# Sample attention of a decoder step: which load is asked for first, products side by side in the array, and the LayerNorm's columns

## What is computed

```python
q, k, v = project(x, w_in)
# LongNet heads: one softmax over the 1024 cached and 8 new rows, 8 heads of 64
o_A = dilated_attention_sample(q_a, cat(cache_a_k[b], k_a), cat(cache_a_v[b], v_a))
# NSA heads, 2 KV heads, three branches
k_c, v_c = compress_rows(pages of cmp_k, w1_k, w2_k), compress_rows(pages of cmp_v, w1_v, w2_v)
o_cmp, p = compressed_attention(q_raw, k_c, v_c)
idx      = select_blocks(p)                      # 16 of 17 blocks of 64 rows
o_sel    = selected_attention(q_rot, pages of sel_k, sel_v through page_table[b], idx)
o_win    = window_attention_sample(q_rot, cat(win_k[b], k_w), cat(win_v[b], v_w))
o_B      = g0*o_cmp + g1*o_sel + g2*o_win
x = LayerNorm(alpha*x + cat(o_A, o_B) @ w_o)
x = LayerNorm(alpha*x + PEER(x))                 # product-key experts
```

## Time and profile before

| what | value |
|---|---|
| median of 3 runs | 1405.68 us (1404.91 to 1408.95) |
| the profiled execution | 1406.61 us, its span 1404.7 us |
| mean granted TensorE clock | 0.981 of full |
| busy over the span | PE 95%, DVE 67%, ACT 42%, POOL 20% |
| DMA | 359.05 MB, mean 256 GB/s |
| sample attention | from 304.6 to 460.6 us of the span |

### The profile page before, as it was taken

How to read it: one execution, slowest core, us unless ns; L and a number is a source line. 1 busy time by engine, 2 the same in 40 slices (tenths; PEclk the granted TensorE clock), 3 DMA queues, 4 the chain that set the end, 5 groups by cost and what they waited for, 6 DMA issues and landing times.

```text
span 1404.7 us, 26191 instructions
## 1 busy us (share of the span) xinstructions
PE 1332.6 (95%) x8743; PEld 1121.0 (80%) x8744; DVE 945.5 (67%) x2191; ACT 589.1 (42%) x1048; POOL 276.3 (20%) x491
## 2 busy tenths in 40 slices
PE   9989999988888999998999999999999999999995
PEld 6869788864545466787998988999988999889895
DVE  3451334334442239998998888887888888888886
ACT  4423777623332121112333545445454444454444
POOL 0004222110000017771111121111121121212201
PEclk9999999998999999999999999999999999999998
DMA  7747676459887416576893999899989899999962
GB/s 249 254 124 252 235 241 219 153 184 352 297 295 287 159 60 231 209 238 211 242 261 123 332 319 315 309 311 320 315 307 320 310 323 315 311 318 310 318 214 81
DMA packets 157471, 359.05 MB, mean 256 GB/s; under 512 B 50515, under 2 KB 92179, under 8 KB 153683
## 3 DMA queue, kind: packets, MB, share of 16 engines
q1 hardware_dynamic: 125682, 240.68, 50.6%
q0 software_dynamic: 24512, 110.84, 22.8%
q10 hardware_dynamic: 7200, 6.56, 1.5%
HBM read 341.82 MB, written 53.35 MB: 281 GB/s over the span
## 4 chain that ended last, share of the span: by engine, by line
PE 49%; DVE 3%; issue 1%; DVEq 1%; ACT 0%; POOLq 0%; POOL 0%
PE psum L1674 25%; PE psum L1664 6%; PE psum L1663 6%; PE psum L1662 6%; PE psum L1687 2%; PE psum L1184 2%; DVE gated_i L1818 2%; DVEq L1818 0%; DVE OT L1814 0%; DVE ln_bn L1124 0%; DVE products L1823 0%; DVE x L1119 0%; DVE v_lo L1831 0%; DVE x L1139 0%; DVE gated_lo L1867 0%
## 5 line engine op out<-in xcount | busy, mean ns | idle before, releaser
L1664 PE MATMUL psum<-x_hi,u_lo 128*128 128x256 f32 x760 | 215.1, 283 | 0.0
L1663 PE MATMUL psum<-x_lo,u_hi 128*128 128x256 f32 x760 | 215.0, 283 | 0.0
L1662 PE MATMUL psum<-x_hi,u_hi 128*128 128x256 f32 x760 | 214.6, 282 | 0.0
L1831 DVE TENSOR_TENSOR v_lo<-big,v_hi 128x1024 fp32r<-128x1024 f32 x128 | 156.7, 1224 | 35.3 <-ACT v_hi L1742 33.9
L1742 ACT ACTIVATE v_hi<-big 128x1024 fp32r<-128x1024 f32 x128 | 135.2, 1057 | 84.2 <-PE psum L1674 79.5
L1674 PE MATMUL psum<-v_hi,gated_hi 128*128 128x512 f32 x512 | 159.4, 392 | 4.3 <-DVE gated_lo L1867 4.3
L1674 PE MATMUL psum<-v_lo,gated_hi 128*128 128x512 f32 x512 | 158.4, 390 | 0.0
L1674 PE MATMUL psum<-v_hi,gated_lo 128*128 128x512 f32 x512 | 158.0, 390 | 0.0
L1663 PEld LDWEIGHTS psum<-x_lo,u_hi 128*128 128x128 f32 x760 | 145.5, 191 | 3.7
L1662 PEld LDWEIGHTS psum<-x_hi,u_hi 128*128 128x128 f32 x760 | 145.5, 191 | 3.7
L1664 PEld LDWEIGHTS psum<-x_hi,u_lo 128*128 128x128 f32 x760 | 145.5, 191 | 0.0
(11 more groups left out here) (304 smaller groups left out, 2422.0 us busy)
## 6 DMA issues: line engine op xcount, KB each, us to landing
big<-in_peer_v SPq DMA_DIRECT2D x128, 512.0 KB
big<-in_peer_u SPq DMA_DIRECT2D x116, 512.0 KB, 5.1
big<-in_a_k SPq DMA_DIRECT2D x8, 2048.0 KB, 11.9
a_vals<-in_a_v SPq DMA_DIRECT2D x8, 2048.0 KB
keep_ak<-in_a_k POOLq DMA_DIRECT2D x32, 508.0 KB, 5.7
keep_av<-in_a_v POOLq DMA_DIRECT2D x24, 512.0 KB, 5.5
wq_ring<-in_peer_wq SPq DMA_DIRECT2D x16, 512.0 KB, 4.6
gate_w<-gate_matrix SPq DMA_DIRECT2D x8, 1024.0 KB, 15.2
```

The lines of the kernel that those rows point to most:

```text
L1662: pe.matmul(H[:, 0:SEQ], uh[:, q, kc], x1h[:, k, :], start=(k == 0), stop=False)
L1663: pe.matmul(H[:, 0:SEQ], uh[:, q, kc], x1l[:, k, :], start=False, stop=False)
L1664: mm = pe.matmul(H[:, 0:SEQ], ul[:, q, kc], x1h[:, k, :], start=False, stop=(k == KD - 1))
L1831: ve.tensor_tensor(vl[:, q], vs[:, q], vh[:, q].bitcast(F32), ALU.subtract).then_inc(s["v_lo"], 1)
```

## The change

1. **Loads ahead of the block.** `load_sel_pages` moves out of `attention_block`, and `pg` becomes a tile of its own that is there in `compress_block` already. SP asks for the pages of batches 0 and 1 behind the last compression page. ScalarE's queue issues none. `w1k` and `w1v` and the two slots of `va` share one tile (`t.wide`), so the LongNet values of batch 0 are asked for in the compression too, once `w1k` has been read for the last time (`cmp_hid` at 28).
2. **SP's order.** In the block SP asks for the rest of the values of 0, the values of 1, keys of 2, and then, for b = 2 to 7, keys of b+1, pages of b, values of b. The two halves of w_o stand where keys of 8 and 9 would.
3. **Pairs.** The two page-score products of a batch go to columns 0 to 63 and 64 to 127 of the array (PSUM partitions 0 to 63 and 64 to 127 of two banks), and both banks are waited for ahead of them. In `values` the window and compressed products go to the upper half and are written between the eight page products. VectorE reads them from there.
4. **Outputs.** `turn_out(b - 2)` stands behind `sel_scores(b)`.
5. **LayerNorm.** `LEFT` is a list by tile: 640 for the first LayerNorm as before, and 384, 704, 640 for tiles 0, 1, 2 of the second. The sample tile's steps move to k = 0 to 3.

```diff
+def load_sel_pages(eng, t, d, s, b):
+
+    for p in range(PAGES):
+        r = eng.value_load(t.ptab[0:1, b * PAGES + p:b * PAGES + p + 1], min_val=0, max_val=79)
+        eng.dma_start(t.pg[:, b % 2, p].rearrange("p a n -> p (a n)"),
+                      d.sel_pool[bass.ds(r, 1)].rearrange("a p n -> p (a n)")).then_inc(s[f"ld_pg{b % 2}"], 16)
...
+            for x in range(2):
+                load_sel_pages(sp, t, d, s, x)
+            sp.wait_ge(s["cmp_hid"], 2 * NK)
+            sp.dma_start(t.va[:, 0].rearrange("p j n -> p (j n)"), d.a_v[0]).then_inc(s["ld_v0"], 16)
...
-        va = sb("a_vals", [P, 2, 8, 512])
-        pg, kw = sb("sel_pages", [P, 2, PAGES, 2, P]), t.kw
+        va = t.va
+        pg, kw = t.pg, t.kw
...
         bank = lambda i: t.psum[:, i]
         chunk = lambda b, n: 6 * b + n
 
-        def load_sel_pages(eng, b, places):
-
-            for p in places:
-                r = eng.value_load(t.ptab[0:1, b * PAGES + p:b * PAGES + p + 1], min_val=0, max_val=79)
-                eng.dma_start(pg[:, b % 2, p].rearrange("p a n -> p (a n)"),
-                              d.sel_pool[bass.ds(r, 1)].rearrange("a p n -> p (a n)")).then_inc(s[f"ld_pg{b % 2}"], 16)
 
         @block.sync
         def _(sp):
-            for b in range(NB):
-                q = b % 2
-                if b >= 2:
+            wo = t.big[:].rearrange("p (k n) -> p k n", k=KD)
+
+            def keys(b):
+                if b < NB:
                     sp.wait_ge(s["s_scores"], chunk(b - 2, 3) + 1)
-                if b >= 2:
-                    sp.dma_start(ka[:, q], d.a_k[b]).then_inc(s[f"ld_ka{q}"], 16)
-                    sp.dma_start(kw[:, q], d.w_k[b]).then_inc(s[f"ld_ka{q}"], 16)
-                    sp.wait_ge(s["s_sel_used"], b - 1)
-                load_sel_pages(sp, b, range(PAGES // 2 if b == 0 else 0, PAGES))
+                    sp.dma_start(ka[:, b % 2], d.a_k[b]).then_inc(s[f"ld_ka{b % 2}"], 16)
+                    sp.dma_start(kw[:, b % 2], d.w_k[b]).then_inc(s[f"ld_ka{b % 2}"], 16)
+                else:
+                    x = b - NB
+                    sp.wait_ge(s["s_scores"], chunk(b - 2, 3) + 1)
+                    for k in range(4 * x, 4 * x + 4, 2):
+                        sp.dma_start(wo[:, k:k + 2], d.w_o[:, k:k + 2]).then_inc(s[f"ld_wo{x}"], 16)
+
+            def vals(b):
+                q, o = b % 2, SEQ + NT * b
                 if b >= 2:
                     sp.wait_ge(s["s_pv"], b - 1)
-                sp.dma_start(va[:, q].rearrange("p j n -> p (j n)"), d.a_v[b]).then_inc(s[f"ld_v{q}"], 16)
+                if b:
+                    sp.dma_start(va[:, q].rearrange("p j n -> p (j n)"), d.a_v[b]).then_inc(s[f"ld_v{q}"], 16)
                 sp.dma_start(vw[:, q].rearrange("p j n -> p (j n)"), d.w_v[b]).then_inc(s[f"ld_v{q}"], 16)
-                o = SEQ + NT * b
                 sp.dma_start(vn[:, q, 0:512], d.o_av[o:o + NT, :]).then_inc(s[f"ld_v{q}"], 16)
                 sp.dma_start(vn[:, q, 512:768], d.o_kv[o:o + NT, 256:512]).then_inc(s[f"ld_v{q}"], 16)
 
-            wo = t.big[:].rearrange("p (k n) -> p k n", k=KD)
-            for k in range(0, KD, 2):
-                if k == 0 or k == 4:
-                    sp.wait_ge(s["s_scores"], chunk(NB - 2 + k // 4, 3) + 1)
-                sp.dma_start(wo[:, k:k + 2], d.w_o[:, k:k + 2]).then_inc(s[f"ld_wo{k // 4}"], 16)
+            vals(0)
+            vals(1)
+            keys(2)
+            for b in range(2, NB):
+                keys(b + 1)
+                sp.wait_ge(s["s_sel_used"], b - 1)
+                load_sel_pages(sp, t, d, s, b)
+                vals(b)
+            keys(NB + 1)
...
             def sel_scores(b):
                 q = b % 2
                 pe.wait_ge(s[f"ld_pg{q}"], 16 * PAGES * (b // 2 + 1))
+                o = [chunk_begin(b, 4 + x) for x in range(2)]
                 for x in range(2):
-                    o = chunk_begin(b, 4 + x)
-                    pe.matmul(o[0:64, :], qn[:, 1, b, :], pg[:, q, 4 * x:4 * x + 4, 0, :], start=True, stop=True).then_inc(s["s_scores"], 1)
+                    pe.matmul(o[x][64 * x:64 * x + 64, :], qn[:, 1, b, :], pg[:, q, 4 * x:4 * x + 4, 0, :], start=True, stop=True).then_inc(s["s_scores"], 1)
 
             def turn(b, n):
 
...
                 if b >= 2:
                     pe.wait_ge(s["s_normed"], b - 1)
                 o = bank(5 + q)
+                sel, win, cmp = o[0:64, 2 * P:3 * P], o[64:P, 3 * P:4 * P], o[64:P, P:2 * P]
                 for j in range(8):
-                    mm = pe.matmul(o[0:64, 2 * P:3 * P], zB[:, q, j, :], pg[:, q, j, 1, :], start=(j == 0), stop=False)
-                mm.then_inc(s["s_sel_used"], 1)
-                pe.matmul(o[0:64, 2 * P:3 * P], zB[0:NT, q, 12, :], vn[:, q, 512:640], start=False, stop=True)
-                pe.matmul(o[0:64, P:2 * P], pcT[:, b, :], t.vc[:, b, :], start=True, stop=True)
-                for j in range(4):
-                    pe.matmul(o[0:64, 3 * P:4 * P], zB[:, q, 8 + j, :], vw[:, q, j, :], start=(j == 0), stop=False)
-                pe.matmul(o[0:64, 3 * P:4 * P], zB[0:NT, q, 13, :], vn[:, q, 640:768], start=False, stop=True)
+                    mm = pe.matmul(sel, zB[:, q, j, :], pg[:, q, j, 1, :], start=(j == 0), stop=False)
+                    if j == 7:
+                        mm.then_inc(s["s_sel_used"], 1)
+                    if j < 4:
+                        pe.matmul(win, zB[:, q, 8 + j, :], vw[:, q, j, :], start=(j == 0), stop=False)
+                    if j == 4:
+                        pe.matmul(win, zB[0:NT, q, 13, :], vn[:, q, 640:768], start=False, stop=True)
+                    if j == 5:
+                        pe.matmul(cmp, pcT[:, b, :], t.vc[:, b, :], start=True, stop=True)
+                pe.matmul(sel, zB[0:NT, q, 12, :], vn[:, q, 512:640], start=False, stop=True)
                 for j in range(9):
                     for c in range(4):
                         w, v = (zA[:, q, j, :], va[:, q, j, :]) if j < 8 else (zAn[:, q, :], vn[:, q, 0:512])
...
                 if 1 <= b <= NB:
                     for n in range(4):
                         turn(b - 1, n)
+                if b < NB:
+                    sel_scores(b)
                 if b >= 2:
                     turn_out(b - 2)
-                if b < NB:
-                    sel_scores(b)
                 if 1 <= b <= NB:
                     values(b - 1)
 
...
-            load_sel_pages(act, 0, range(PAGES // 2))
...
-                ve.tensor_scalar(z, o[0:64, P:2 * P], gs[:, b, 0:1], None, ALU.mult).then_inc(s["s_branch"], 1)
+                ve.tensor_scalar(z, o[64:P, P:2 * P], gs[:, b, 0:1], None, ALU.mult).then_inc(s["s_branch"], 1)
...
-                                                 bank(chunk(b, 4 + x) % 3)[0:64].rearrange("p (j n) -> p j n", n=64), SCALE, m, ALU.mult, ALU.add))
+                                                 bank(chunk(b, 4 + x) % 3)[64 * x:64 * x + 64].rearrange("p (j n) -> p j n", n=64), SCALE, m, ALU.mult, ALU.add))
...
-LEFT = 640
+LEFT = [640, 640, 640, 384, 704, 640]
...
-        s, c = self.s, slice(0, LEFT)
+        s, c = self.s, slice(0, LEFT[self.first + i])
...
                         body(i, i * UP + (UP * FIRST * half + k), k, i * 6 + (6 * FIRST * half + plain(k)), half)
             for k in range(UP):
                 body(POS - 1 - FIRST, NE - UP + k, k, NU - 6 + plain(k), 1, UP - k)
-                if k == 3:
+                if k == 1:
                     norm.root(act, 2)
-                if k == 6:
+                if k == 2:
                     norm.scale(act, 2)
             for i in range(2):
                 norm.root(act, i)
...
                 if k == 0:
                     ve.wait_ge(s["values"], 65)
                     ve.tensor_copy(low, acc[64:P]).then_inc(s["y_low"], 1)
-                if k == 1:
                     ve.wait_ge(s["y_low"], 1)
                     ve.tensor_tensor(low, low, acc[0:64], ALU.add).then_inc(s["y_low"], 1)
-                if k == 3:
+                if k == 1:
                     ve.wait_ge(s["y_low"], 2)
                     norm.moments(ve, 2)
-                if k == 5:
+                if k == 2:
                     ve.wait_ge(s["ld_ln2"], 32)
                     norm.centre(ve, 2)
-                if k == 6:
                     norm.factors(ve, 2)
+                if k == 3:
                     norm.left(ve, 2)
             for i in range(2):
                 ve.wait_ge(s["y_done"], i + 1)
...
+        t.wide = ab("w1_then_a_vals", [P, 2, 4096])
+        t.w1k, t.w1v = [t.wide[:, x].rearrange("p (c n) -> p c n", c=CMP_W1) for x in range(2)]
+        t.va = t.wide[:].rearrange("p q (j n) -> p q j n", j=8)
...
-            t.w1k, t.w1v = cb("w1k", [P, CMP_W1, 256]), cb("w1v", [P, CMP_W1, 256])
...
+            t.pg = att.enter_context(nc.sbuf_tensor("sel_pages", [P, 2, PAGES, 2, P], F32, side="right"))
```

14 lines of the change are left out of this document (7 added, 7 removed).

## The result

The changed kernel takes 1395.27 us (median of 4 runs, 1394.48 to 1396.73), the one before 1405.43 beside it: a ratio of 0.9924, interval 0.9905 to 0.9942. It is faster, by 10.2 us and not by the 24.4 that I forecast, and it lies outside my range (1373 to 1392). Two later measurements of the same kernel on other chips gave 0.9909 (0.9888 to 0.9930) and 0.9897 (0.9877 to 0.9917), 12.9 and 15.1 us; their medians, 1391.3 and 1391.9, lie just inside the range. So the sign was right and the size off by 9 to 14 us.

The account below looks back on a forecast made before the run. The prediction took TensorE's waits in sample attention, chiefly for late keys behind SP's single queue, as the bound. Start 3.7, period 16.4, tail 2.9 and end 1.8 sum to 24.8: 1406.6 to 1381.8, 1381.0 for the median; range 1373 to 1392.

Parts of the forecast that it names:

- The round trip of a page slot: Six batches: signal, issuing, landing and products around one page slot take 15.75 us, or 17.2 at the low clock.
- The loads ahead: Compression: issuing 16 pages and one set of values there costs nothing.
- The early steps of the sample tile: End of the kernel: moving these steps takes 1.4 us off, against 0.5 of new wait.
- The period: Six batches of sample attention: 16.5 us each where they took 19.2, so 16.4 us less in all.
- the limit of the bytes: Six batches: 99.2 us of full DMA queue for their loads limits each to 16.5 us.
- the second rival: Six batches: the pairs don't overlap, the round trip grows to 18.0 us, so 1393.5 us; chance 0.06.
- The first rival: Six batches: the clock falls in every batch, period 17.2 us or a little more, so 1387 us; chance 0.22.
- My other sum, 15.7: Six batches: by two observed DMA rates, keys and values take 11.4 us and pages 4.3, together 15.7 a batch.
- The start: Start of the attention block: early loads and the pairs of batches 0 and 1 bring 3.7 us.
- The tail: Behind the last batch: pairs and outputs bring 2.9 us, between 1.7 and 4.
- The end: Last normalization: the new split of columns brings 0.9 us, part of 1.8 for the end of the kernel.
- The third rival: Whole block: only the first loads pay and the period stays near 19 us, so about 1397 us; chance 0.05.

Follow-up runs that it names:

- e16: The changed kernel repeated with no edit, on another chip: 1391.85 us, ratio 0.9897 to the kernel before.
- e4: Changed kernel with ScalarE's queue issuing four of the eight pages from batch 2 on and SP the other four: 1378.31 us, ratio 0.9817.
- e2: Changed kernel with the pages of batches 0 and 1 and the values of batch 0 asked for in the block again: 1404.27 us, ratio 1.0001.
- e13: Changed kernel with 16 unused transposes on TensorE ahead of the page scores of batches 2 to 7: 1385.84 us, ratio 0.9862.
- e7: Changed kernel with the pairs undone, scores and values on rows 0 to 63 one after the other: 1391.26 us, ratio 0.9897.
- e14: Changed kernel with pages issued from two queues and 512 columns on VectorE for tile 0 of the last normalization: 1379.63 us, ratio 0.9804.
- e6: Changed kernel with the end undone, 640 columns for all tiles and the sample tile's steps at their old places: 1393.68 us, ratio 0.9909.
- e1: The changed kernel repeated with no edit: 1391.28 us, ratio 0.9909 to the kernel before.
- e3: Changed kernel with SP's order undone, keys of b+1 behind pages and values of b: 1400.31 us, ratio 0.9962.
- e11: Changed kernel with pages from two queues, grouped pairs, turned outputs ahead of the page scores and 512 columns for tile 0: 1383.79 us, ratio 0.9868.
- e12: Changed kernel with pages from two queues, values without pairs, turned outputs ahead of the page scores and 512 columns for tile 0: 1390.99 us, ratio 0.9912.
- e18: Changed kernel with pages from two queues, 512 columns for tile 0, 16 unused transposes and grouped pairs: 1377.24 us, ratio 0.9795.
- e9: Changed kernel with only the turned outputs put back ahead of the page scores: 1390.69 us, ratio 0.9902.

## Why the prediction was wrong

**What held.** The waits for keys went and waits for pages took their place, of about 2 us in each batch of the result's profile, of 0.3 to 2.5 in five of six in e16. The round trip of a page slot is the limit (e4). The loads ahead cost the compression nothing (e2, e16). At the start TensorE waits for VectorE and for no load. The early steps of the sample tile are worth 1.0 net of their new wait (forecast 0.9), and the new wait of 0.47 is my 0.5.

**The period, 16.4 forecast and 11.5 measured (9.9 in e16).** This is the step that failed: 16.5 us for a period. It is 4.9 of the 12.6 us by which the result's profile misses my 24.8, and 6.5 of the 7.0 in e16. I took it where the limit of the bytes stood and in the middle of the trip's 15.75 to 17.2. The first is no limit (below), and the trip is at the upper end, since in the changed kernel the low clock stands behind nearly every wait for pages. By the trip of the result (391.85 to 409.01):

- Page products 4.0 for my 1.9. I took 1.9 from the row of sixteen products alone, while the pairs put the window products, the 8-row ones and the compressed one ahead of the signal: 3.0 at the full clock (e13). The low clock adds the other 1.0.
- Page scores and turned outputs 2.0 for my 1.35; 1.5 at the full clock (e13).
- Issuing 8.4 for my 8.6, and the landing 1.8 for my 3.0. The last page's own wait is shorter than the median from issue to landing.
- The time until SP wakes, 0.9 in both.

In sum 17.2 for my 15.75. At the full clock the errors in the order and in the landing (1.1 too little, 1.2 too much) cancel: the six batches of e13 average 15.8, so my 15.75 was right there by luck. These six gain 20.4 us (115.4 to 95.0), more than the 16.4 that I forecast. What kept the changed kernel at 11.5 is thus above all the low clock, which I had left to a rival.

I had written that the pairs "are inside that period and don't add to it"; they do, and I had it only in the second rival, where they don't overlap at all. The pairs themselves overlap as L933's evidence said: a pair every 0.11 us, as one product alone. What they save goes into the changes between heights: each piece of two records takes 0.36 us (394.14 to 394.50), where two in a run of sixteen take 0.24 (1.96 by 8, e7). The Trainium skill, TensorEngine Tiling (Array Packing), Key Properties, which the prediction set against the pairs, names a drain at a change of mode, and the trace agrees that something is paid there.

**The clock.** The first rival was the case: the wait moves to the pages and the slow products stand right behind it. Period 17.2 or a little more, I wrote; measured 17.3 over the six. I gave it 0.22 because 1.59 us of idle time had left the clock full and only 3.03 had not the earlier trace rows. These two rows were too thin to set the odds by, and the trace of before had others. Behind a wait of 1.08 us for VectorE it has the page scores at 3.38 us, where they take 1.93 at the full clock, and the same behind 1.09 at 415.81:

```profile
360.52 0.33 PE L940 MATMUL psum<-c,rope_then_samples 128*128 128x128 f32 x1 [1.08 <-DVE rope_then_samples L1056]
360.98 3.38 PE L889 MATMUL psum<-sel_pages,rope_then_samples 128*64 128x512 f32 x4
```

The length of a wait doesn't decide it either. In the result's profile 1.8 to 2.3 us brought the low clock in each batch, and 1.37 did in e14; but behind 1.89 us in e6 and 1.91 in e7 the whole turn kept a clock of 1.00:

```profile
337.02 1.08 PE L905 MATMUL psum<-sel_pages,rope_then_samples 128*64 128x512 f32 x4 [1.89 <-DMA sel_pages<-in_sel_pool]
```

So a wait of 1 to 2 us here is a risk of the low clock and not a certainty. The Trainium skill, TensorE: Matmul & The Clock Gate, HAM oscillation, describes a loop that waits for a DMA in each round and so starts each round slow. The waits of its example are longer (about 3 to 5 us), but for the odds of this rival the loop is the same, and the runs agree that such a loop loses the clock (0.82 in e16 against 0.99 in e13 over the same hundred microseconds). What I had of its price was also too small: 1.4 us a batch by L879's rows. The turn of batch 7, where the low clock lasted through all the values, takes 19.7 us and is 3.2 of the 4.9 missed; in e16 three turns of the six are like it.

**The limit of the bytes, 16.5, was no limit.** I got it from the time times the share, 99.2 us of full queue for six batches. The share counts an engine as busy also while it handles pages that arrive one by one at 0.50 for 147 GB/s. With two queues 5.8 MB a batch pass in 14.4. Nor were all of those bytes the batches': 321 GB/s for 115.4 us are 37.0 MB, 2 MB more than six times 5.8, since the loads of w_o begin at 432.83; without them the same sum gives 15.5. My other sum, 15.7 from two rows of rates, was nearer, and wrong in the same way.

**The start, 3.7 forecast.** 2.0 in the result's profile, 3.3 in e16 and e1. The difference between them is mostly how long the low clock lasts: TensorE waits 3.56 us for VectorE in batch 1 in both, and in the result's profile the window scores behind it are slow too (L898, 1.97 for 1.07).

**The tail, 2.9 forecast.** 2.3 in both.

**The end, 0.9 for the columns.** 0.1. The two times 0.27 less of VectorE were there, but a larger share for GpSimd in tile 0 reaches into the centring of tile 1, which takes 1.66 instead of 0.94. I had used just this effect for `gated_lo` and did not look for it where my own term put two such operations side by side.

**The rest.** 2.6 in the compression go with the low clock there, and part of 1.1 in the last stretch may; in e16 both fall in the other direction (-0.3 and -1.9). By e16's profile the changed kernel gained 17.8 us, by the result's 12.2; the medians on three chips say 10.2, 12.9 and 15.1. The third rival (only the first loads pay, 1397) came nearest by its number, but by e3 not by its mechanism. The long periods of e14 (20.3 and 19.8 us) have short waits (1.4 and 1.7) and a clock of 0.68 and 0.74, those of e11 a late page and a clock of 0.82 and 0.83. What stays open: what decides whether a wait of 1 to 2 us brings the low clock, and how long it then lasts.

## What to carry to other kernels

When a wait is removed, write down the loop that closes behind it as a trip with all its parts (signal, issue, landing, use) and read each part in the order in which the changed code runs it, for a signal counts from everything that stands ahead of it. If TensorE will idle in every round, take the low clock as the forecast and not as a rival, and look through the whole trace of before for the waits that brought it; a little work with no use in the wait can pay, and issuing gathered pages from two queues pays more. With two queues, look at which page is issued behind a large load. A period times the DMA share is no lower bound of the bytes' time when part of the loads are issued one by one.

## What was not expected of the hardware

- 16 transposes of 1.9 us with no use, ahead of a wait that then is at most 1.5 us, hold the granted clock at 0.99 where it was 0.82, and take 6 us off the kernel (e13).
- Eight pages issued from SP take 8.0 to 8.6 us in all but one of the turns (10.7, e2); from SP and ScalarE at once 3.5 to 4.5 for four each. Halving the issue took 13 us off, the largest gain of any edit here. A page of ScalarE's that is issued just behind SP's 2 MB of values lands in 8.8 to 9.7 us in five of six cases (e11, e12, e18).
- A VectorE operation with two inputs in SBUF beside a GpSimd one takes 1.66 us for 0.94, or 1.23 for 0.42; an overlap of 0.1 us instead of 0.9 is enough to be rid of it (e14).
- TensorE can fall to 1.2 GHz behind a wait of 1.08 us (before) and keep the full clock behind one of 1.91 (e7). The turns of one kernel then take 13.6 to 20.4 us (e16).
- The same program reaches the same barrier at 304.3, 305.5 or 307.2 us (and variants of it at up to 308.8) by where the low clock falls. The waits of TensorE on the way, those over 0.2 us summed, don't follow it: 15.6 us in all at 308.8 (e3), 16.2 at 304.4 (e9). Differences of 3 us between single profiles say nothing unless the clock of the stretch is compared.
